# One plain pair of output tiles at the start of each seven-product feed-forward stage

## What is computed

```
h = h + 0.5 * (silu(x @ w_gate) * (x @ w_up)) @ w_out     x = rmsnorm(h, g)
h = h + mixer(rmsnorm(h, g'))       retention + pooling; short convolution + gated delta rule
h = h + 0.5 * (feed-forward again)
```

## Time and profile before

| | us |
|---|---|
| median of 3 runs | 2238.92 |
| the profiled execution | 2239.0 |
| its span | 2237.2 |
| PE busy | 2153.8 (96%) |
| DVE busy | 1630.6 (73%) |
| ACT busy | 914.9 (41%) |
| POOL busy | 214.2 (10%) |

### The profile page before, as it was taken

One profiled execution on the slowest core, in us unless ns is written; L12 is line 12 of the kernel. 1 busy time (PEld: TensorE's weight loads), 2 busy tenths in 40 slices (PEclk: granted clock), 3 DMA queues, 4 the chain that ended last, 5 costly groups with the idle time before them and its releaser, 6 DMA issues.

```text
span 2237.2 us, 31602 instructions
## 1 busy us (share of the span) xinstructions
PE 2153.8 (96%) x13144; PEld 1932.3 (86%) x13144; DVE 1630.6 (73%) x1826; ACT 914.9 (41%) x1131; POOL 214.2 (10%) x167
## 2 busy tenths in 40 slices
PE   4999999999999998999998699999999997999998
PEld 4998998888777887998997699899788887998997
DVE  7984885453466548984887997497688768984983
ACT  5541443232233335541443444244483255541443
POOL 0000001630123001000002300000102102000002
PEclk9999999999999999999999899999999998999999
DMA  3332332333222222332341133233221122341341
GB/s 118 104 128 71 105 132 69 111 113 103 76 85 76 85 94 89 110 126 73 104 132 47 57 110 127 74 106 114 78 74 66 57 79 82 104 133 66 104 133 48
DMA packets 58894, 210.47 MB, mean 94 GB/s; under 512 B 6528, under 2 KB 8832, under 8 KB 58496
## 3 DMA queue, kind: packets, MB, share of 16 engines
q1 hardware_dynamic: 58320, 205.30, 27.6%
q0 software_dynamic: 288, 2.62, 0.3%
q10 hardware_dynamic: 144, 0.52, 0.1%
HBM read 206.33 MB, written 2.10 MB: 93 GB/s over the span
## 4 chain that ended last, share of the span: by engine, by line
PE 89%; DVE 7%; ACT 2%; issue 1%; DMA 0%; DVEq 0%; ACTq 0%
PE accs L660 24%; PE accs L661 24%; PE accs L662 24%; PE mixbs L662 4%; PE mixbs L660 4%; PE mixbs L661 4%; DVE w_lo L1725 2%; DVE xc_f L1760 1%; PE mixbs L1168 1%; PE mixbs L1191 1%; ACT w_hi L1252 1%; PE accs L1129 1%; PE accs L1128 1%; PE accs L1130 1%; DVE w_raw L1713 1%
## 5 line engine op out<-in xcount | busy, mean ns | idle before, releaser
L1252 ACT ACTIVATE w_hi<-w_raw 128x1024 fp32r<-128x1024 f32 x516 | 535.2, 1054 | 668.2 <-PE accs L662 290.3
L1725 DVE TENSOR_TENSOR w_lo<-w_raw,w_hi 128x1024 fp32r<-128x1024 f32 x516 | 641.0, 1245 | 110.6 <-ACT w_hi L1252 104.2
L660 PE MATMUL accs<-xc_hi,w_hi 128*128 128x256 f32 x1760 | 509.3, 289 | 63.0 <-DVE w_lo L1725 37.9
L661 PE MATMUL accs<-xc_lo,w_hi 128*128 128x256 f32 x1760 | 506.3, 288 | 0.0
L662 PE MATMUL accs<-xc_hi,w_lo 128*128 128x256 f32 x1760 | 506.0, 288 | 0.0
L660 PEld LDWEIGHTS accs<-xc_hi,w_hi 128*128 128x128 f32 x1760 | 346.5, 197 | 68.3 <-DVE w_lo L1725 43.0
L661 PEld LDWEIGHTS accs<-xc_lo,w_hi 128*128 128x128 f32 x1760 | 346.7, 197 | 0.5
L662 PEld LDWEIGHTS accs<-xc_hi,w_lo 128*128 128x128 f32 x1760 | 346.4, 197 | 0.0
L660 PE MATMUL accs<-hid_hi,w_hi 128*128 128x512 f32 (+1 forms) x714 | 277.4, 389 | 6.4 <-DVE w_lo L1725 6.4
L661 PE MATMUL accs<-hid_lo,w_hi 128*128 128x512 f32 (+1 forms) x714 | 276.8, 388 | 0.0
L662 PE MATMUL accs<-hid_hi,w_lo 128*128 128x512 f32 (+1 forms) x714 | 276.6, 387 | 0.0
(11 more groups left out here) (385 smaller groups left out, 3029.4 us busy)
## 6 DMA issues: line engine op xcount, KB each, us to landing
w_raw<-weights SPq DMA_DIRECT2D x384, 512.0 KB, 3.4
y_t<-h SPq DMA_DIRECT2D x16, 128.0 KB, 1.8
h<-x_t SPq DMA_DIRECT2D x3, 512.0 KB, 7.0
k1c<-const POOLq DMA_DIRECT2D x1, 1536.0 KB, 7.4
k2c<-const POOLq DMA_DIRECT2D x1, 1024.0 KB, 7.1
h<-x_t ACTq DMA_DIRECT2D x1, 512.0 KB, 5.3
cst<-const SPq DMA_DIRECT2D x1, 161.0 KB, 8.8
...
```

The lines of the kernel that those rows point to most:

```text
L660: pe.matmul(bank, w_hi[:, n % HI_SLOTS, w], hi, start=start, stop=False, skip_group_check=read_between)
L661: pe.matmul(bank, w_hi[:, n % HI_SLOTS, w], lo, start=False, stop=False, skip_group_check=read_between)
L1252: act.activation(w_hi[:, n % HI_SLOTS, :], w_raw[RAW[n]][:, :], ACT.Copy).then_inc(hi_split, 1)
L1725: dve.tensor_tensor(w_lo[LO[n]][:, :], w_raw[RAW[n]][:, :], w_hi[:, n % HI_SLOTS, :].bitcast(F32), ALU.subtract).then_inc(lo_split, 1)
```

## The change

`NPLAIN = (1, 1, 1, 1)`: the first double of each network's first half is plain. It has 4 blocks in place of 7 (gate, up, gate, up; each 8 tiles x 3 matmuls of 512 columns), uses `x_hi` and `x_lo`, makes no weight sums, and leaves its four PSUM banks with `gate_plain` and `up_plain`. The other ten doubles keep seven products. Their P1, P2, P3 now read quarters of `x_hi` and `x_lo`; only P6, P7, P5, P4 read combinations, in new tiles `xm_hi` and `xm_lo` with four places instead of seven.

Ahead of a feed-forward network a tile gets only `x_hi`, `x_lo`, its square, and on ACT one copy a pair (`twin`). The combinations are made during the plain double: `mix_tokens` and `mixed_rest` on DVE, `round_mixed` on ACT, put in between the splits, the norm's chain and the four evacuations in `plain_first`. POOL's scaling of `h` in ffn2 waits for them. In ffn0 the first weight block and the first part of `x` come in smaller transfers (`BEGIN` is 256 of the block's 1024 columns, the first two parts of `x` are one tile each). Buffers are laid out anew; there are eight for weights as before.

```diff
+NPLAIN = (1, 1, 1, 1)
+PHASES = [("ffn0_in0", 42 - 3 * NPLAIN[0]), ("ffn0_out0", 12), ("ffn0_in1", 35), ("ffn0_out1", 10), ("pool_in", 4), ("v", 4), ("pool_in2", 4),
...
 
-X_PARTS = [(0, 2), (2, 4), (4, 6), (6, 8)]
+BEGIN = 2 * P
+X_PARTS = [(0, 1), (1, 2), (2, 4), (4, 6), (6, 8)]
 
...
+            def operands(i, k):
+
+                even, odd = 2 * k, 2 * k + 1
+                if i == P1:
+                    return x_hi[:, even, t1], x_lo[:, even, t1]
+                if i == P2:
+                    return x_hi[:, odd, t1], x_lo[:, odd, t1]
+                if i == P3:
+                    return x_hi[:, odd, t2], x_lo[:, odd, t2]
+                x = {P6: T2, P7: U3, P5: U1, P4: U4}[i]
+                return xm_hi[:, k, x, :], xm_lo[:, k, x, :]
...
+            def plain_first(f, n, a):
+
+                r = FFN_NORM[f]
+                for k in range(KD):
+                    pe.wait_ge(x_done, KD * r + k + 1)
+                    if f == 0 and k == 0:
+                        pe.wait_ge(w_split_begun, 2)
+                    if k == (0 if f else BEGIN // P):
+                        take_block(n)
+                        take_bank(a)
+                    last = product(n, k, acc[0], x_hi[:, k, :], x_lo[:, k, :], k == 0, k == KD - 1)
+                last.then_inc(block_done, 1)
+                dense(n + 1, a + 1, x_hi, x_lo, middle=(lambda: split_sum(f"norm{r}")) if f else None,
+                      at={1: 2, 2: 0, 3: 4}.get(f, 0))
+                if f == 2:
+                    split_sum("norm3b", square2_r)
+                dense(n + 2, a + 2, x_hi, x_lo, middle=None if f else lambda: split_sum("norm0"))
+                dense(n + 3, a + 3, x_hi, x_lo)
...
-                    for i, (d, n0) in enumerate(doubles(f, p)):
-                        quadrants(f, d, n0, OUT0[f"ffn{f}_in{p}"], i == 0)
+                    drain = OUT0[f"ffn{f}_in{p}"]
+                    for i, (d, n0, plain) in enumerate(doubles(f, p)):
+                        if plain and i == 0:
+                            plain_first(f, n0, drain)
+                        elif plain:
+                            for b in range(4):
+                                dense(n0 + b, drain + b, x_hi, x_lo)
+                        else:
+                            quadrants(f, d, n0, drain)
+                        drain = drain + 4 if plain else 0
                     out_tiles(f, p)
...
+            def twin(r, j):
+
+                act.activation(xm_f[:, j, U3, :], h[:, 2 * j + 1, t2], ACT.Copy, scale=vcol(GAIN[r], 2 * j + 1)).then_inc(b22_done, 1)
+
+            def round_mixed(f, j):
+
+                act.wait_ge(x_mixed, 12 * f + 3 * j + 3)
+                act.activation(xm_hi[:, j, T2:U1, :], xm_f[:, j, T2:U1, :], ACT.Copy)
+                act.activation(xm_hi[:, j, U1, :], xm_f[:, j, U1, :], ACT.Copy,
+                               scale=vcol(GAIN[FFN_NORM[f]], 2 * j)).then_inc(xm_hi_done, 1)
...
+                act.wait_ge(*ready)
+                square_of(r, m)
+                if r == 3:
+                    act.wait_ge(chained, m + 1)
+                if r == 6:
+                    act.activation(h[:, m, :], h[:, m, :], ACT.Copy, scale=vcol("final_norm_2", m)).then_inc(y_scaled, 1)
                     return
-                act.activation(xc_f[:, j, U3, :], h[:, m, t2], ACT.Copy, scale=gain).then_inc(xb_hi, 1)
-                act.activation(xc_hi[:, j, B21:B22 + 1, :], h[:, m, :].rearrange("p (t n) -> p t n", t=2), ACT.Copy,
-                               scale=gain).then_inc(xb_hi, 1)
-
...
+            def plain_first(f, d, n0, a):
+
+                r = FFN_NORM[f]
+                if f:
+                    round_norm(r)
+                    split(n0 + 2)
+                if f == 0:
+                    round_norm(0)
+                    for j in range(KD // 2):
+                        twin(0, j)
+                if f == 2:
+                    round_sum("norm3b", sumsq2[:, :], sq2_summed, KD, square2_r)
+                round_mixed(f, 0)
+                split(n0 + 3)
+                round_mixed(f, 1)
+                take_root(f"norm{r}", 1.0 / D, r_one[:, :] if f == 2 else rstd[:, :])
+                if f == 2:
+                    act.wait_ge(h_chain, 1)
+                    act.activation(rstd[:, :], rstd[:, :], ACT.Sqrt, scale=1.0 / D, bias=eps).then_inc(rooted, 1)
+                split(n0 + 4)
+                act.wait_ge(drained, a + 1)
+                silu_plain(d, 0)
+                round_mixed(f, 2)
+                split(n0 + 5)
+                act.wait_ge(drained, a + 3)
+                silu_plain(d, 1)
+                round_mixed(f, 3)
...
+            act.activation(w_hi[:, 0, 0:BEGIN], w_raw[RAW[0]][:, 0:BEGIN], ACT.Copy).then_inc(w_split_begun, 1)
             act.wait_ge(tables_loaded, 16)
-            for i in range(len(X_PARTS)):
+            for i, (begin, end) in enumerate(X_PARTS):
                 act.wait_ge(x_loaded[i], 16)
-                combine(0, 2 * i)
-                combine(0, 2 * i + 1)
-                round_mixed(0, i)
+                for m in range(begin, end):
+                    act.activation(x_hi[:, m, :], h[:, m, :], ACT.Copy, scale=vcol("norm_ffn1", m)).then_inc(x_hi_done, 1)
                 if i == 0:
-                    split(0)
+                    act.wait_ge(loaded[RAW[0]], 16)
+                    act.activation(w_hi[:, 0, BEGIN:], w_raw[RAW[0]][:, BEGIN:], ACT.Copy).then_inc(hi_split, 1)
...
+            def mixed_square(m):
+                act.wait_ge(sq_summed, KD * 5 + m - 1)
+                act.activation(square[:, m % 2, :], h[:, m, :], ACT.Square).then_inc(sq_done, 1)
+
             for m in range(KD):
...
+            def mix_tokens(f, j):
+
+                r = FFN_NORM[f]
+                even, odd = vcol(GAIN[r], 2 * j), vcol(GAIN[r], 2 * j + 1)
+                dve.wait_ge(b22_done, 4 * f + j + 1)
+                dve.scalar_tensor_tensor(xm_f[:, j, U3, :], h[:, 2 * j, t2], even, xm_f[:, j, U3, :], ALU.mult,
+                                         ALU.subtract).then_inc(x_mixed, 1)
+                dve.tensor_tensor(xm_f[:, j, U1, :], h[:, 2 * j, t1], h[:, 2 * j, t2], ALU.subtract)
                 dve.wait_ge(x_mixed, 12 * f + 3 * j + 1)
-                dve.scalar_tensor_tensor(xc_f[:, j, T2, :], h[:, 2 * j, t1], even, xc_f[:, j, U3, :], ALU.mult,
+                dve.scalar_tensor_tensor(xm_f[:, j, T2, :], h[:, 2 * j, t1], even, xm_f[:, j, U3, :], ALU.mult,
                                          ALU.subtract).then_inc(x_mixed, 1)
-                dve.scalar_tensor_tensor(xc_f[:, j, U1, :], h[:, 2 * j, t1], even, xc_f[:, j, U1, :], ALU.mult, ALU.subtract)
                 dve.wait_ge(x_mixed, 12 * f + 3 * j + 2)
-                dve.scalar_tensor_tensor(xc_f[:, j, U4, :], h[:, 2 * j + 1, t1], odd, xc_f[:, j, T2, :], ALU.mult,
+                dve.scalar_tensor_tensor(xm_f[:, j, U4, :], h[:, 2 * j + 1, t1], odd, xm_f[:, j, T2, :], ALU.mult,
                                          ALU.subtract).then_inc(x_mixed, 1)
...
+            def mixed_rest(f, j):
+
+                dve.wait_ge(xm_hi_done, 4 * f + j + 1)
+                dve.tensor_tensor(xm_lo[:, j, T2:U1, :], xm_f[:, j, T2:U1, :], xm_hi[:, j, T2:U1, :].bitcast(F32), ALU.subtract)
+                dve.scalar_tensor_tensor(xm_lo[:, j, U1, :], xm_f[:, j, U1, :], vcol(GAIN[FFN_NORM[f]], 2 * j),
+                                         xm_hi[:, j, U1, :].bitcast(F32), ALU.mult, ALU.subtract).then_inc(xm_done, 1)
+
+            def rest_of(r, m):
+
+                dve.wait_ge(x_hi_done, KD * r + m + 1)
                 dve.scalar_tensor_tensor(x_lo[:, m, :], h[:, m, :], vcol(GAIN[r], m), x_hi[:, m, :].bitcast(F32),
                                          ALU.mult, ALU.subtract).then_inc(x_done, 1)
...
+            def gate_plain(d, n, a, u):
+
+                dve.wait_ge(block_done, n + 1)
+                dve.tensor_tensor(f_gate[:, u, :], acc[2 * u], rstd[:, :], ALU.mult).then_inc(drained, 1)
+
+            def up_plain(d, n, a, u):
+
+                dve.wait_ge(block_done, n + 1)
+                dve.wait_ge(f_acted, 2 * d + u + 1)
+                tile = hid_of(d).start + u
+                dve.tensor_tensor(hid_f[:, tile, :], acc[2 * u + 1], f_gate[:, u, :], ALU.mult).then_inc(drained, 1)
+
+            def plain_first(f, d, n0, a):
+
+                r = FFN_NORM[f]
+                if f:
+                    rest_norm(r)
+                    prepare(n0 + 2)
+                if f == 0:
+                    rest_norm(0)
+                if f == 2:
+                    rest_sum("norm3b", sumsq2[:, :], square2_r)
+                mix_tokens(f, 0)
+                prepare(n0 + 3)
+                mix_tokens(f, 1)
+                mixed_rest(f, 0)
+                invert_root(f"norm{r}", r_one[:, :] if f == 2 else rstd[:, :])
+                if f == 2:
+                    dve.wait_ge(summed, SUM["norm3b"] + 1)
```

(83 more changed lines are left out.)

312 lines of the change are left out of this document (114 added, 198 removed), and 3 rows, old and new, of the table PHASES.

## The result

The changed kernel takes 2212.97 us (median of 4 runs, 2212.68 to 2214.46). The kernel before takes 2238.77 us on the same chip (4 runs, 2238.36 to 2241.32). The ratio is 0.9884 with a 95% interval of 0.9867 to 0.9901: 1.2% faster. The forecast was 2215 with a range of 2198 to 2232.

A forecast was written before the change was run, and what follows sets the result against it. DVE's work at each network's beginning was taken as the bound; gains 13.5 + 4.2 + 1 + 7.7 = 26.4 us, less 2 for the half clock, take 2239.0 to 2214.6, so 2215 us, range 2198 to 2232.

The forecast's parts named there:

- DVE's list: At each network's beginning: DVE's ordered work until PE has two blocks of lead sets the price.
- The seam: Into ffn1 and ffn3: x_lo done 4.2 us later while PE has 4.76 us of work, so no wait.
- the first matmul's bounds: ffn0: first matmul at 7 to 8.5 us; bounds half of 6.1 and 13.9, giving gains of 16 or 8.
- the term that failed: ffn3's beginning to its third double: 50.4 us against 58.15 before, a gain of 7.7.
- mix 0: First mix_tokens (index 0) in the plain double's DVE work; in ffn3 put at 8.9 us, all after it 1.7 later.
- Its 1 us: ffn2's beginning with output blocks ahead: 128 to 131 us against 131.2, gain 0 to 3, taken as 1.
- price of 5.6 us for seven lengthened DVE operations: ffn2's second double: POOL's scaling of h delays P6, P2, P7 by seven DVE operations x 0.8 us.
- bare half-clock stretches: Whole sum: 2 us taken off for PE's half-clock stretches after waits that aren't hidden.
- The beginnings close wholly: Rival: PE's losses at all beginnings vanish, 2147 us, chance 0.04; half of that, 2190 to 2202, chance 0.13.
- POOL and the clock take more: Rival: scalings cost 13.4 us, not 5.6, and 6.8 lies bare in ffn1 and ffn3; 2227 or 2232, chance 0.17.
- The lead is never won back: Rival: later doubles each wait for a late split; 0.66 us over 40 doubles costs 26.4; 2249 at 0.9; chance 0.05.
- Nothing gained: Rival: landings bind ffn0's start and ffn2 loses what the others win; 2235 to 2243 us, chance 0.05.

The follow-up runs named there:

- the third experiment: Changed kernel with only DVE's order altered: up_plain 0 is evacuated before the third mix_tokens and second mixed_rest; 2218.92 us, ratio 0.9909.
- the combined run: Changed kernel plus two plain doubles, root early, POOL's scaling late, square first, fifth block's split ahead of the reciprocal; 2181.60 us, ratio 0.9751.

## Why the prediction was right, and where it was off

**The path.** The theory was that DVE's list until PE has its lead sets a beginning, and PE's own work does not. The runs show it three times: PE started 6.4 us later costs 0.4, a bank freed 2.9 us earlier brings nothing, and 2 us taken out of the list's idle time bring 2.1 to 2.4 us in three networks and 1.3 in ffn1. The second and the third show its limit too: where PE stands just ahead of the products that end the waiting, its half clock adds to the list (in ffn1 about 1.1 us with the bank freed early, 0.8 with the root early). DVE's timeline of ffn1 after, from the reciprocal to what P1 and P6 wait for (compare for the prices):

```profile
868.00 3.35 DVE L1901 RECIPROCAL rstd<-rstd 128x512 f32<-128x512 f32 x1 [2.04 <-ACT rstd L1363]
871.38 0.69 DVE L1923 TENSOR_TENSOR f_gate<-accs,rstd 128x512 f32<-128x512 f32 x1
...
877.17 0.68 DVE L1930 TENSOR_TENSOR hid_f<-accs,f_gate 128x512 f32<-128x512 f32 x1
...
882.41 0.68 DVE L1930 TENSOR_TENSOR hid_f<-accs,f_gate 128x512 f32<-128x512 f32 x1
```

Counted from 852.10, the start of the network, `up_plain` 0 ends at 25.8 (listed: 25.5) and `up_plain` 1 at 31.0 (listed: 30.7). P1 waits 3.5 us (listed 3.3). The second double then lasts 23.23 us, where 23.2 was listed (48.7 - 25.5). P1's loss to the clock lies in P6's wait, as the prediction said; the third experiment is what it looks like when it doesn't. The size of that loss was listed wrongly: 2.9 us, P1 at the half clock throughout, would not have fitted into the listed wait of 2.3. P1 runs at the half clock for 3.41 us of its 4.4, which costs 1.6.

**The seam.** ffn1's first double has PE busy for 22.43 of 25.85 us, and 25.85 less the wait of 3.5 is that: no wait at the seam. The plain double is 4 x 5.44 us.

**ffn0.** First matmul at 7.06 (forecast 7 to 8.5), P1 at 42.74 (41.6), third double at 65.98 (66). The time of the third double is right, in part because 1.2 us were added for the landings, while P1 came 1.1 later than listed; the prediction's words about the first matmul's bounds (a gain of 16 or 8 by when it comes) were wrong, for the run with PE held back shows that this time hardly matters.

**ffn3, the term that failed.** Its 7.7 us measured 5.2. The list was to reach the end of mix 0 8.9 us after the last tile; mix 0 only starts at 9.5. POOL's and ACT's timelines of ffn3's start after:

```profile
1844.33 7.15 POOL L2590 TENSOR_TENSOR sumsq<-sumsq,square 128x512 f32<-128x512 f32 x4 [3.44 <-ACT square L1735]
```
```profile
1851.51 0.63 ACT L1352 ACTIVATE square_r<-sumsq 128x512 fp32r<-128x512 f32 x1 [2.43 <-POOL sumsq L2590]
```
```profile
1852.18 0.69 DVE L1855 TENSOR_TENSOR square_r<-sumsq,square_r 128x512 fp32r<-128x512 f32 x1 [1.84 <-ACT square_r L1352]
...
1854.27 0.48 DVE L1811 SCALAR_TENSOR_TENSOR xm_f<-h,vec,xm_f 128x256 f32<-128x256 f32 x1
```

The prediction put the last square and one addition behind the last tile. The squares trail by a tile there, so POOL had four additions in one piece, 7.15 us, the longest 2.17 (in the view of that tile) where one alone takes 1.30; four of those would be 5.2, so 1.9 us of the piece are additions made longer beside DVE. ACT waited 2.43 us on POOL and DVE 1.84 on ACT, and mix 0 is late by that. With each square ahead of its `x_hi` the additions don't pile up; POOL's timeline of that run:

```profile
1842.54 1.30 POOL L2588 TENSOR_TENSOR sumsq<-sumsq,square 128x512 f32<-128x512 f32 x1 [2.63 <-ACT square L1735]
...
1846.23 1.30 POOL L2588 TENSOR_TENSOR sumsq<-sumsq,square 128x512 f32<-128x512 f32 x1 [0.71 <-ACT square L1735]
```

The last addition ends at 1847.5 in place of 1851.5, mix 0 starts 6.4 us after the last tile in place of 9.5, and ffn3 gains the same 3.1 us. So the step that was listed wrongly is the norm's part ahead of mix 0: a wait on POOL that was put at one addition.

**ffn2.** Its 1 us measured 3.1, but 128 was the low end of the list (128 to 131) and 1 a choice inside it. The steps came as listed: last `x_lo` 68.2 after the start of the output blocks (69.1), the first root at 81.7 (82.5), gate 0 at 92.1 (92.8), P1 at 98.1 (98.6). POOL's scaling started at 101.4 (102). DVE and POOL there:

```profile
1249.40 15.51 POOL L2606 TENSOR_TENSOR h<-h,r_one 128x512 f32<-128x512 f32 x8 [32.11 <-DVE xm_f L1818]
```
```profile
1257.04 2.29 DVE L1789 TENSOR_TENSOR w_lo<-w_raw,w_hi 128x1024 fp32r<-128x1024 f32 x1
...
1263.69 0.68 DVE L1999 TENSOR_TENSOR f_gate<-accs,f_s 128x512 f32<-128x512 f32 x1
```

The price of 5.6 us for seven lengthened DVE operations came out as 6.8 for the double (30.08 against 23.24 without POOL).

**The clock.** 2 us were taken off for bare half-clock stretches. The second double was listed at 23.2 us without such a loss, and it lasts 23.24 in ffn0, 23.23 in ffn1, 23.24 in ffn3, and 23.24 in ffn2 once POOL's scaling is out of it. So no such loss lies bare there, and the term was not needed. The sum was forecast as 24.4 and 25.8 were measured. That it came so close is partly luck: ffn3 was 2.5 us too high and ffn2 2.1 too low, and the two nearly cancel.

**The rivals.** *The beginnings close wholly* fell: four waits for `hid_f`, 22.4 us, are there. Two plain doubles close ffn1, and the combined run ffn1 and ffn3. *POOL and the clock take more* (a POOL operation holds a DVE operation for its whole length, 13.4 us) fell: 6.8. *The lead is never won back* fell: the doubles from the third on last 20.16 us, with DVE busy for 19.25 of it in ffn0's third. *Nothing gained* fell: ffn0 gained 13.5 us, and ffn2 gained 3.1 where it was to lose.

What stays open: what the last 6.4 us at ffn2's seam would cost to remove; which of POOL's eight operations held which DVE operation, since the view gives their sum; and how much of ffn0's gain is due to the smaller transfers.
